# Rows by groups of 128 tokens, x parts for two tiles at once, low-part products behind the high ones

## The reference, cut to what matters

```python
x = layer_norm(x, ln_in_g, ln_in_b)          # 2048 prompt and 32 sample tokens, 1024 wide
proj = x @ w_in[l]                           # 1024 -> 9 * 256 columns
xa, ga, xb, gb, gc, q, k, v, xp = jnp.split(proj, 9, axis=-1)
...                                          # four mixers: RG-LRU, gated conv, stick-breaking attention, pooling
out = jnp.concatenate([ya, yb, yc, yd], axis=-1) @ w_out
x = layer_norm(ALPHA * x + mix, ln1_g[l], ln1_b[l])
x = layer_norm(ALPHA * x + sq_relu_mlp(x, w_ff1[l], w_ff2[l]), ln2_g[l], ln2_b[l])
```

## Time and profile before

| | |
|---|---|
| median of 3 runs | 2453.49 us (2453.25 to 2456.35) |
| the profiled execution, its own time | 2453.47 us |
| its span, first to last instruction | 2451.9 us |
| TensorE matmul busy | 2410.5 us, 98% of the span |
| TensorE weight loads busy | 2330.7 us, 95% |
| VectorE busy | 1587.5 us, 65% |
| ScalarE busy | 1287.9 us, 53% |
| GpSimd busy | 242.4 us, 10% |
| mean granted TensorE clock | 0.997 |

### The profile page before, as it was taken

One profiled execution on the slowest core, in us unless ns is written; L12 is line 12 of the kernel. 1 busy time (PEld: TensorE's weight loads), 2 busy tenths in 40 slices (PEclk: granted clock), 3 DMA queues, 4 the chain that ended last, 5 costly groups with the idle time before them and its releaser, 6 DMA issues.

```text
span 2451.9 us, 36722 instructions
## 1 busy us (share of the span) xinstructions
PE 2410.5 (98%) x13263; PEld 2330.7 (95%) x13263; DVE 1587.5 (65%) x2234; ACT 1287.9 (53%) x1981; POOL 242.4 (10%) x526
## 2 busy tenths in 40 slices
PE   7999999999999999999999999999999999999998
PEld 7999999999999999999999999999999999999998
DVE  7535662656777787777778777757755665863335
ACT  5466523545656745556555566554445555444432
POOL 0011320200101100111100011000122130000000
PEclk9999999999999999999999999999999999999999
DMA  8434554533444434444443443433566674343332
GB/s 256 152 110 140 165 170 131 168 120 127 160 126 157 130 117 140 131 149 141 122 131 124 130 146 115 133 115 117 173 192 183 203 238 140 117 136 120 112 115 86
DMA packets 141526, 351.64 MB, mean 143 GB/s; under 512 B 20625, under 2 KB 64146, under 8 KB 141218
## 3 DMA queue, kind: packets, MB, share of 16 engines
q1 hardware_dynamic: 128994, 312.88, 40.2%
q0 software_dynamic: 12352, 36.42, 4.7%
HBM read 300.11 MB, written 49.12 MB: 142 GB/s over the span
## 4 chain that ended last, share of the span: by engine, by line
PE 92%; DVE 3%; ACT 2%; issue 1%; DMA 1%; SPq 0%; DVEq 0%; ACTq 0%
PE PS L1133 21%; PE PS L1135 21%; PE PS L1134 21%; PE PS L871 5%; PE PS L869 5%; PE PS L870 5%; PE PS L939 2%; PE PS L961 1%; PE PS L960 1%; PE PS L929 1%; PE PS L1023 1%; PE PS L930 1%; PE PS L1053 1%; PE PS L1011 1%; PE PS L909 1%
## 5 line engine op out<-in xcount | busy, mean ns | idle before, releaser
L1433 ACT ACTIVATE w_hi_lo<-w_raw 128x1024 fp32r<-128x1024 f32 x240 | 253.0, 1054 | 282.8 <-PE PS L1135 276.7
L1133 PE MATMUL PS<-a_hi,w_hi_lo 128*128 128x416 f32 x1080 | 385.0, 356 | 1.9 <-DVE a_lo L2185 1.9
L1135 PE MATMUL PS<-a_hi,w_hi_lo 128*128 128x416 f32 x1080 | 378.9, 351 | 0.0
L1134 PE MATMUL PS<-a_lo,w_hi_lo 128*128 128x416 f32 x1080 | 378.1, 350 | 0.0
L1986 DVE TENSOR_TENSOR w_hi_lo<-w_raw,w_hi_lo 128x1024 fp32r<-128x1024 f32 x240 | 292.7, 1220 | 57.2 <-ACT w_hi_lo L1433 54.9
L1133 PE MATMUL PS<-h_hi,w_hi_lo 128*128 128x416 f32 x824 | 294.3, 357 | 0.0
L1135 PE MATMUL PS<-h_hi,w_hi_lo 128*128 128x416 f32 x824 | 289.8, 352 | 0.0
L1134 PE MATMUL PS<-h_lo,w_hi_lo 128*128 128x416 f32 x824 | 288.9, 351 | 0.0
L2013 DVE TENSOR_TENSOR h_lo<-h_full,h_hi 128x416 fp32r<-128x416 f32 x160 | 94.6, 592 | 224.1 <-ACT h_hi L1448 223.9
L1133 PEld LDWEIGHTS PS<-a_hi,w_hi_lo 128*128 128x128 f32 x1080 | 202.8, 188 | 5.4 <-DVE a_lo L2185 2.8
L1134 PEld LDWEIGHTS PS<-a_lo,w_hi_lo 128*128 128x128 f32 x1080 | 203.3, 188 | 2.1
(11 more groups left out here) (334 smaller groups left out, 5206.4 us busy)
## 6 DMA issues: line engine op xcount, KB each, us to landing
w_raw<-w_all SPq DMA_DIRECT2D x380, 512.0 KB, 3.5
proj_scratch<-stage SPq DMA_DIRECT2D x70, 208.0 KB, 2.0
k_rows<-kv_out SPq DMA_DIRECT2D x80, 128.0 KB, 4.1
v_hi_lo<-v_scratch SPq DMA_DIRECT2D x40, 256.0 KB, 4.3
x_scratch<-x_full SPq DMA_DIRECT2D x20, 416.0 KB, 2.7
x_residual<-x_scratch SPq DMA_DIRECT2D x5, 1664.0 KB, 7.8
pages<-ck SPq DMA_DIRECT2D x64, 128.0 KB, 2.2
pages<-ck POOLq DMA_DIRECT2D x64, 128.0 KB, 2.6
```

What stands on the lines that cost most here:

```text
L1133: pe.matmul(out, w_h, mh_[:, k, :], start=(g == 0), stop=False)
L1134: pe.matmul(out, w_h, ml_[:, k, :], start=False, stop=False)
L1135: ins = pe.matmul(out, w_l, mh_[:, k, :], start=False, stop=(g == KT - 1))
L1433: act.activation(halves(w_hi(n)), raw_halves(n), ACT.Copy).then_inc(s_wh, 1)
```

## The change

Row groups are 128, 128, 128 and 32 tokens, one transfer each. The raw tiles 2 and 3 go to a place of their own, so that their loads wait for nothing. `block_back` rounds two tiles in one ScalarE pass and subtracts two in one VectorE pass. In block 0 the first tile's scaling is VectorE's. In the first two steps the sixteen low-weight products come after all the others. All low parts of weights are VectorE's: 0, 1 and 2 behind block 0's x parts, 3 between `block_var(1)` and `block_nmr(1)`. TensorE gets four plain float32 matmuls on zeros as soon as the third group of rows is there. In step 3 the transposes of block 1 are each half a step later.

```diff
+GROUPS = [(a, min(a + P, BLK)) for a in range(0, BLK, P)]
...
             def load_raw(p):
-                if p >= 2:
-                    sp.wait_ge(s_wl, p - 1)
+                if p in (2, 3):
+                    spare = x23[:, 1, p - 2, :, :].rearrange("p k t -> p (k t)")
+                    sp.dma_start(spare[:, 0:KT * P], w_all[AT[PORD[p]]]).then_inc(s_raw2[p - 2], 16)
+                    return
+                if p >= 4:
+                    sp.wait_ge(s_wl, p - 3 if p < 6 else p - 1)
...
             def load_rows(b):
-                for j in range(NR):
-                    at = b * BLK + j * ROW
-                    for first, last in ROW_PARTS:
-                        sp.dma_start(x_rows(b)[first:last, j, :], x_all[at + first:at + last]).then_inc(
-                            s_xin[b % 2] if b else s_xr0[j], 16)
+                for j, (first, last) in enumerate(GROUPS):
+                    sp.dma_start(x_rows(b)[0:last - first, j, :], x_all[b * BLK + first:b * BLK + last]).then_inc(
+                        s_xin[b % 2] if b else s_xr0[j], 16)
...
             load_raw(2)
+            load_raw(3)
             for k in range(0, KT, 2):
                 store_x1(0, k)
-            load_raw(3)
             load_rows(2)
...
                     for p in range(2):
                         if k == 0:
-                            pe.wait_ge(s_wl, p + 1)
+                            pe.wait_ge(s_wh, p + 1)
...
                         pe.matmul(out, w_h, x_hi(0)[:, k, :], start=(k == 0), stop=False)
                         pe.matmul(out, w_h, x_lo(0)[:, k, :], start=False, stop=False)
-                        ins = pe.matmul(out, w_l, x_hi(0)[:, k, :], start=False, stop=(k == KT - 1))
-                        if k == KT - 1:
-                            ins.then_inc(s_pst, 1)
+                for p in range(2):
+                    pe.wait_ge(s_wl, p + 1)
+                    for k in range(KT):
+                        ins = pe.matmul(PS[:, p, 0:BLK], w_at(wp_lo(p), k), x_hi(0)[:, k, :], start=False, stop=(k == KT - 1))
+                    ins.then_inc(s_pst, 1)
+
+            pe.wait_ge(s_zero, 1)
+            pe.wait_ge(s_xr0[2], 16)
+            for _ in range(4):
+                pe.matmul(PS[:, 7, 0:BLK], x23[:, 0, 0, 0, 0:P], x23[:, 0, 0, 0, :], start=True, stop=True)
...
+                    if b or p >= 2:
+                        project(b * GRP + p, turned=range(4) if b == 0 and p == 3 else ())
                     if b == 0 and p == 3:
-                        for k in range(4):
+                        for k in range(4, KT):
                             turn_back(1, k)
-                    if b or p >= 2:
-                        project(b * GRP + p, turned=range(4, KT) if b == 0 and p == 3 else ())
...
             def block_back(b, ks):            # ScalarE
                 for k in ks:
-                    if k % 2 == 0:
+                    if k % 2 == 0 and (b or k):
...
+                    elif k % 2:
                         wait_apart(act, s_xfa, b * 4 + k // 2 + 1)
-                    else:
                         act.wait_ge(s_xfd, b * 4 + k // 2 + 1)
-                    act.activation(x_hi(b)[:, k, :], x_full(b, k), ACT.Copy).then_inc(s_xh, 1)
+                        act.activation(x_hi(b)[:, k - 1:k + 1, :], x_full(b, k - 1, 2), ACT.Copy).then_inc(s_xh, 2)
...
             split_hi(2)
+            split_hi(3)
             put_out(0)
             put_out(1)
-            split_hi(3)
...
             def block_back(b, ks):            # VectorE
                 for k in ks:
                     if k % 2:
+                        if b == 0 and k == 1:
+                            dve.wait_ge(s_bt, 1)
+                            dve.tensor_scalar(x_full(0, 0), PS[:, 4, 0:BLK], ln_gb[:, 0, 0:1], ln_gb[:, 1, 0:1], ALU.mult,
+                                              ALU.add).then_inc(s_xfa, 1)
...
-                        for d in (k - 1, k):
-                            dve.wait_ge(s_xh, b * KT + d + 1)
-                            dve.tensor_tensor(x_lo(b)[:, d, :], x_full(b, d), x_hi(b)[:, d, :].bitcast(F32), ALU.subtract).then_inc(s_xl, 1)
+                        dve.wait_ge(s_xh, b * KT + k + 1)
+                        dve.tensor_tensor(x_lo(b)[:, k - 1:k + 1, :], x_full(b, k - 1, 2), x_hi(b)[:, k - 1:k + 1, :].bitcast(F32),
+                                          ALU.subtract).then_inc(s_xl, 2)
...
             dve.memset(gsel[:, :, :, :], 0.0).then_inc(s_mzero, 1)
+            dve.memset(x23[:, 0, 0, 0, :], 0.0).then_inc(s_zero, 1)
+            own.up(dve.memset(mv[:, :, :], 1.0))
             block_var(0)
             block_nmr(0)
-            split_lo(0)
             dve.wait_ge(s_const, 32)
             block_back(0, range(KT))
-            dve.wait_ge(s_wl, 2)
-            split_lo(2)
+            for p in range(3):
+                split_lo(p)
             block_var(1)
+            split_lo(3)
             block_nmr(1)
-            split_lo(3)
...
         def _(pool):
-            pool.wait_ge(s_wl, 1)
-            pool.wait_ge(s_wh, 2)
-            pool.tensor_tensor(halves(wp_lo(1)), raw_halves(1), halves(wp_hi(1)).bitcast(F32), ALU.subtract).then_inc(s_wl, 1)
```

More of the change, by code:

```diff
@@ L321, in build @@
         with ExitStack() as e1:
-            sb_at("x2_and_x3", [P, 2, 2, KT, BLK], F32, X_AT, e1)
+            x23 = sb_at("x2_and_x3", [P, 2, 2, KT, BLK], F32, X_AT, e1)
             rows_b = sb("rows_b", [P, NR, D], F32, e1)
@@ L425, in halves, with raw_at, raw_in_halves @@
             return bass.AP(w[0], w[1] * HALF, [[WT, P], [ODD, 2], [P, KT // 2], [1, P]])
+        def raw_at(n):
+            return raw[:, n % 2, :]
+        def raw_in_halves(p):
+            if p not in (2, 3):
+                return raw_halves(p)
+            spare = x23[:, 1, p - 2, :, :].rearrange("p k t -> p (k t)")
+            return spare[:, 0:KT * P].rearrange("p (k h c) -> p h k c", h=2, c=P)
         def raw_halves(n):
-            return raw[:, n % 2, :].rearrange("p (k h c) -> p h k c", h=2, c=P)
+            return raw_at(n).rearrange("p (k h c) -> p h k c", h=2, c=P)
         def w_at(w, k):
@@ L438, in build @@
         s_raw = [sem("raw_in0"), sem("raw_in1")]
+        s_raw2 = [sem("raw_2_in"), sem("raw_3_in")]
+        s_zero = sem("zeros_made")
         s_wh, s_wl = sem("w_hi_made"), sem("w_lo_made")
@@ L845, in turn_back @@
                     pe.wait_ge(s_xfd if k % 2 else s_xfa, b * 4 + (k - 4) // 2 + 1)
-                for j in range(NR):
-                    ins = pe.transpose(PS[:, 4 + k % 4, j * ROW:(j + 1) * ROW], x_rows(b)[0:ROW, j, k * P:(k + 1) * P],
-                                       ident[0:ROW, 0:ROW])
+                for j, (first, last) in enumerate(GROUPS):
+                    n = last - first
+                    ins = pe.transpose(PS[:, 4 + k % 4, first:last], x_rows(b)[0:n, j, k * P:(k + 1) * P], ident[0:n, 0:n])
                 ins.then_inc(s_bt, 1)
@@ L1264, in split_hi @@
             def split_hi(p):
-                act.wait_ge(s_raw[p % 2], 16 * (p // 2 + 1))
+                if p in (2, 3):
+                    act.wait_ge(s_raw2[p - 2], 16)
+                else:
+                    act.wait_ge(s_raw[p % 2], 16 * max(p // 2, 1))
                 if p >= 4:
@@ L1284, in block_norm @@
                 for j, width in ((0, D), (2, D // 2)):
-                    row = x_rows(b)[0:ROW, j, 0:width]
-                    act.activation(row, row, ACT.Identity, bias=nmr[0:ROW, j:j + 1], scale=rstd[0:ROW, j:j + 1]).then_inc(s_nat, 2)
+                    row = x_rows(b)[:, j, 0:width]
+                    act.activation(row, row, ACT.Identity, bias=nmr[:, j:j + 1], scale=rstd[:, j:j + 1]).then_inc(s_nat, 2)
             def block_back(b, ks):
                 for k in ks:
-                    if k % 2 == 0:
+                    if k % 2 == 0 and (b or k):
                         act.wait_ge(s_bt, b * KT + k + 1)
@@ L1686, in split_lo, with size @@
                 dve.wait_ge(s_wh, p + 1)
-                dve.tensor_tensor(halves(wp_lo(p)), raw_halves(p), halves(wp_hi(p)).bitcast(F32), ALU.subtract).then_inc(s_wl, 1)
+                dve.tensor_tensor(halves(wp_lo(p)), raw_in_halves(p), halves(wp_hi(p)).bitcast(F32), ALU.subtract).then_inc(s_wl, 1)
+            def size(j):
+                return GROUPS[j][1] - GROUPS[j][0]
             def block_var(b):
                 if b:
-                    dve.wait_ge(s_xin[b % 2], 32 * NR * (b // 2 + b % 2))
+                    dve.wait_ge(s_xin[b % 2], 16 * NR * (b // 2 + b % 2))
                 for j in range(NR):
                     if b == 0:
-                        dve.wait_ge(s_xr0[j], 32)
+                        dve.wait_ge(s_xr0[j], 16)
                     for h in range(2):
-                        ins = dve.bn_stats(bn[0:ROW, j, h, :], x_rows(b)[0:ROW, j, h * 512:(h + 1) * 512])
+                        ins = dve.bn_stats(bn[0:size(j), j, h, :], x_rows(b)[0:size(j), j, h * 512:(h + 1) * 512])
```

(13 more changed lines are left out.)

10 lines of the change are left out of this document (5 added, 5 removed).

## The result

The changed kernel takes 2470.26 us (median of 4 executions, 2467.96 to 2473.09), the kernel before 2454.35 (2453.25 to 2456.35) on the same chip: ratio 1.0065, 95% interval 1.0052 to 1.0078. It is slower, as forecast, but by 15.9 us where the forecast said 6.1, and outside the range (2456.5 to 2463.0). The profiled execution took 2467.96 us, 14.5 more than that of before. It was the shortest of the four; the other three have a mean granted clock of 0.994 or 0.995 where it has 0.997, so part of the 1.7 to 5.1 us that they took longer may be the clock's, which no trace shows.

A forecast was written before the change was run, and what follows sets the result against it. VectorE's list was taken to bound up to block 2's transposes, TensorE after. Rows +0.73, first scaling -0.77, pairs and low parts +3.22, split_lo(3) +0.27, queue -0.17, block 1's pairs +2.82: +6.10 on 2453.47, 2459.6 us; range 2456.5 to 2463.

The forecast's parts named there:

- VectorE's list: VectorE's work from first statistics to block 2's transposes, said to have no slack and to set the time: +6.10 us.
- The warm-up: Four TensorE matmuls from 10.1 us, done by 15.7: no cost; the 1.2 us gained ends in the wait for pairs.
- Everything behind follows TensorE's queue with its own dense work, so that delay is the change of the time.: Behind block 2's transposes TensorE's work was taken as dense, so their delay of 6.10 us is the whole change.
- The pair period: In block_back, scaling, rounding and subtracting a pair run strictly in sequence: 2.60 us per further pair, +2.82 per whole block.
- The hand-overs: Gaps between scaling, rounding and subtraction of a pair on VectorE and ScalarE, put at 0.04 us each.
- The late low parts: Weight subtractions 0 to 2 before block 1's statistics, 1.13 us each (statistics +3.18), and split_lo(3) later, +0.27.
- The rows: At the start, the last group's passes queue behind the third group's, moving block 0's transposes from 15.56 to 16.29: +0.73 us.
- Overlapping pairs: Rival: VectorE's own passes set the pair period in blocks 0 and 1, 5.8 us less, 2453.8; chance 0.12.
- TensorE was the bound: Rival: up to block 2's transposes TensorE, not VectorE, sets the time, so -2.4 us, 2451.1, faster; chance 0.07.
- The cover of blocks 3 and 4 breaks: Rival: pair period of 2.97 us makes VectorE's line outgrow TensorE's in the later blocks: 2463.2 us; chance 0.10.
- The chances: Slower by over 0.2% was given 0.74 (forecast less 0.04, plus broken cover), within 0.23, faster 0.03.

The follow-up runs named there:

- a_112: The changed kernel with all its edits, but row groups of 112, 112, 96 and 96: 2460.94 us, ratio 1.0031.
- a_full: The changed kernel, but the fourth group of 32 rows transposed over all 128 partitions, 96 of them zeros: 2461.72 us, ratio 1.0031.
- a_by_group: The changed kernel, but where four x tiles are turned together, from block 1 on, their transposes go group by group: 2463.17 us, ratio 1.0039.
- b_groups: The kernel before with row groups of 128, 128, 128 and 32 alone (loads, passes, transposes): 2464.15 us, ratio 1.0039.
- b_pairs_busy: The kernel before with pair passes and 11 more products, results unread, ahead of block 2's first turn: 2459.82 us.
- a_single_112: The changed kernel with single passes per x tile instead of pairs and row groups of 112, 112, 96 and 96: 2453.57 us, ratio 1.0000.
- b_pairs: The kernel before with the pair passes alone: 2460.41 us, ratio 1.0026.
- a_nowarm: The changed kernel without the four warm-up matmuls: 2469.97 us, ratio 1.0060.
- b_112_96: The kernel before with row groups of 112, 112, 96 and 96, one row load a group: 2454.20 us, ratio 1.0002.

## Why the prediction was off

**What held.** VectorE's list sets the transposes of block 2, and these wait 2.4 us for it (forecast 2.8). Pairs are strictly sequential, with passes of 0.90 and 1.02 (0.89 and 1.02). The statistics of block 1 start at 31.18 (31.31). The warm-up costs nothing that shows. From block 2's statistics to its first turn are 8.45 us (8.49). Where the small tiles are taken out, the kernel takes 2460.94 for the 2459.6 of the sum, though two misses nearly cancel in it (`a_112`).

**The step that failed: "Everything behind follows TensorE's queue with its own dense work, so that delay is the change of the time."** The forecast took everything behind block 2 to be TensorE's own dense work, unchanged in length. But the change rewrites each tile's transposes, from four of 104 rows to three of 128 and one of 32, and this edit had no term in the sum, not even a bound; where the forecast asked whether blocks 3 and 4 are covered, it put TensorE's stretch at the 15.03 us of the kernel before, and it is 16.24 (68.67 to 84.91). The new shapes cost 1.20 us for each turn of four tiles, 7.2 us for the six from block 2 on, where TensorE is the bound and nothing covers it. About 0.29 of the 1.20 is the width of the large ones (`a_full`), the rest the way to a small tile and back (`a_by_group`). With pairs alone measured at +6.6 and groups alone at +10.4, the forecast priced the smaller half. The other half of the step, that what is late at the start is late at the end, held to about 2 us. Behind block 4's last turn the profiled execution of the changed kernel is 14.2 us late, and it took 14.5 longer; in `b_groups` these are 10.2 and 11.8, in `a_112` 6.3 and 7.3, in `b_pairs_busy` 5.3 and 5.4.

The Trainium skill, "TensorEngine Tiling (Array Packing)", section "Key Properties", says that changing the tiling mode drains TensorE, and its section "Available Configurations" lists row tilings of 64 and of 32 rows. The runs fit that: tiles of 64 and 32 rows cost (7.19 and 7.22 us from turn to turn) and of 96 or 112 don't (6.03). That such a mode is what these transposes change, no trace shows.

**The terms that were mis-sized.** The pair period: 2.60, measured 2.74. The hand-overs were put at 0.04 each, from where one engine's rounding seemed to start in a group of two; between engines they are 0.10: scaling ends at 17.51, rounding starts at 17.61 and ends at 18.51, the subtraction starts at 18.61. Over the four pairs of block 1 that is 0.57 of the 1.05 us by which block 2 was later than forecast. Another 0.47 is the slow transposes themselves, since the first odd scaling stands 42.03 - 40.64 = 1.39 behind them, not 0.92. In block 0 the same two terms were offset by the earlier rows.

**The late low parts.** The forecast's terms for them are in the sum. With single passes they cost nothing, as VectorE's waits of 0.43 and 0.80 us and GpSimd's pass beside it go in exchange: from block 0's first turn to block 2's are 38.66 us in `a_single_112` and 38.74 before. Beside pairs the edits other than pairs and small tiles cost 1.9 us on that stretch (45.57 in `a_112`, 43.63 in `b_pairs`), and an earlier first turn hides it (14.94 against 16.61).

**The rows.** Forecast +0.73, measured -0.18 in the changed kernel's profiled execution (first turn at 15.38), outside the bounds of 0 and +1.21. The landing was counted by rows from transfers of 96 and 8 rows, and the third group of 128 was put at 10.09. In the seven profiled executions with this division and one transfer a group, its statistics start between 7.39 (`a_nowarm`) and 9.23 (the changed kernel), a spread of 1.8 us between executions with the same loads. Over all profiled executions the sign is clear: block 0's first turn is at 13.57 to 15.38 in the eleven with one transfer a group, and at 15.56 to 16.61 in the three with two (the kernel before, `b_pairs`, `b_pairs_busy`). So undivided row loads bring the start forward, by 1.8 us on the average of these. No run changes the loads alone; `b_112_96`, which changes the division with them, comes nearest.

**The rivals.** Overlapping pairs (2453.8) are out by the period of 2.74. "TensorE was the bound" (2451.1) is out by the wait before block 2. "The cover of blocks 3 and 4 breaks" (2463.2) came nearest in time and wrong in cause: the cover broke not because VectorE's line grew to 21.4, but because TensorE's grew to 23.4.

**The chances.** Slower by over 0.2% adds up to 0.67 - 0.04 + 0.10 = 0.73, not 0.74.

## What to carry to other kernels

When an edit changes the shape of an instruction that the bound engine repeats, price that instruction before anything else, even if the amount of data is the same; if no row shows the new shape, that is a bound to be named and not a zero. On TensorE keep the rows of a transpose in groups of 96 or more (between 64 and 96 nothing was measured; 416 is better cut 4 x 104 than 3 x 128 + 32), or put the small ones of several tiles side by side. And fusing two passes of two engines that take turns saves their fixed cost (0.90 and 1.02 us for a pair, where two single ones take 1.10 and 1.18) but gives up the overlap, which here was worth more (a period of 2.74 against 1.84 us).

## What the runs showed of the hardware

- A 32-row transpose among larger ones costs TensorE 0.23 us for each tile there and back (0.91 for four, `a_full`), with 0.17 us of it a gap before the 32-row weight load; with 64 rows the turn is as long (7.19 us) and the gap 0.14. The load itself is as long as a full one: in the stretch from 60 to 110 us

```profile
L864 PEld LDWEIGHTS PS<-ident,rows_a 128*128 128x128 f32 x33 | 3.6, 140 | 3.1 <-ACT rows_a L1310 2.7
L864 PEld LDWEIGHTS PS<-ident,rows_a 32*128 32x128 f32 x10 | 1.3, 134 | 1.7 <-issue 1.7
```

(groups by shape: busy, mean ns, idle before). Turning 96 rows of zeros along is cheaper than not turning them.
- Behind a short wait the granted clock can fall to 0.50: in the profiled execution with single passes it was 0.50 from 56 to 62 us behind a wait of 1.58 us and the transposes after it, and in that of `a_by_group` 0.51 from 52 to 54 us behind waits of 0.91 and 1.34 us with six products between them. In other executions it stayed at 1.00 behind 2.35 to 2.55 us. At the start the opposite is seen: the pitch is the slow one (32 transposes in 8.63 us) while the column of the granted clock says 1.00.
